# Moved fills, split waits, other banks and a changed order in a one-core transformer layer

## The chip, the core and the metric

One core of a Trainium2 chip runs one launch of a whole layer in f32. The metric is device time in microseconds (us). A core has TensorE (matmuls into eight banks of PSUM), VectorE, ScalarE and GpSimd (elementwise work), and SyncE (SP), which issues most transfers. Each works through its own queue in order and waits on semaphores.

## The reference, cut to what matters

1024 tokens of width 1024. After a layer norm, one projection feeds four token mixers A to D and four gates for each channel; each mixer's output is projected (`w_br_*`), weighted with its sigmoid gate, the four are added, and `w_out` follows. Then a layer norm (LN1), and a mixture of experts: each token takes 6 of 64 experts, and a shared expert runs for all.

```python
def hybrid_mixer(h, w_in, ...):
    proj = h @ w_in
    ...
    g = sigmoid(gate).reshape(bsz, seq, N_BRANCH, D_MODEL)
    merged = g[:,:,0]*(ya @ w_br_a) + g[:,:,1]*(yb @ w_br_b) + g[:,:,2]*(yc @ w_br_c) + g[:,:,3]*(yd @ w_br_d)
    return merged @ w_out

def forgetting_attention(q, k, v, f_logit):            # mixer D
    c = cumsum(log_sigmoid(f_logit))
    s = q @ k.T * HEAD_DIM ** -0.5 + c[query] - c[key]  # causal softmax, then @ v

def moe_ffn(h, ...):
    idx, w = route(xf, w_router, router_bias)           # top 4 of 8 groups, top 6 of 64
    routed = routed_experts(xf, idx, w, wg, wu, wd)     # silu(x @ wg) * (x @ wu) @ wd * w
    shared = (silu(xf @ sg) * (xf @ su)) @ sd
    return routed + shared
```

## The kernel before, in words

All order is written by hand: every engine has its own program, and semaphores tie them together. The stages are these.

**Projection in.** `norm_in_and_project` normalizes and turns the tokens, then projects. Six blocks of 256 columns are done with seven half-size products each instead of eight (`block_part(n, r)`, L767). These need sums of token halves, t1 to t4, which VectorE makes once (L663 to L668), and sums of weights, which GpSimd makes. The semaphore `tsum` counts the token sums.

**Mixers.** A, B, C and D run one after the other. Dense work lies between the small steps of each as a filler. In `mix_d` it is eleven gate units of seven products, each product four *parts* (`gate_part`, L1709): 308 parts in one list. `fill(8, "start")` does the first eight; then TensorE waits for mixer C's output to be read, for rows of ones, and for `drop_in`, the four small copies by SP that put the cumulated forget row into the keys. `score(u)` follows for 32 pairs of row tile and head, with `fill(4)` behind each score, 4 or 3 ahead of each `values`, and 2 within the turns that have two groups. What is left goes last, `fill(len(parts), "end")`. VectorE (`join`) and ScalarE (`copy`) read the products out of the banks, at points that the table `done` gives them from the same fills; GpSimd adds one of them (`crossed`) and makes the weight sums of the unit after next; SP stores the results in DRAM (`gates`, `spilled`) and loads the next weights.

**Merge.** A barrier of all engines. `merge` walks 64 gates in the order `order`: 60 come back from DRAM, four are projected here. SP first loads the four branch weights, a to d. Before the first branch product (L1957) TensorE projects two units and then waits for all four loads, `wbr` at 64.

**LN1, shared expert and routing.** Another barrier, then `norm_and_route`, for eight row tiles m. `mix(m, h)` (L2119) is `w_out`; its result stands in banks 0 and 1, and `mix(m, 0)` waits until VectorE has added tile m-1 into `base` (L2243). Then come the normalization, `turn`, `logits`, `count`, and the shared expert's `up`, `turn_hidden`, `down` (L2167, L2174, L2183), four or five tiles behind. On VectorE these have `hidden` (L2273) between up and turn_hidden, and `sum_base` (L2266) after down. At the stage's end the first experts' lists are made: TensorE `lists(b)` (L2598), VectorE `select` (L2923, what `lists` reads) and `index` (L2928 to L2945, which the gather on GpSimd reads). `turned_first` is the transpose (L2975) of the first gathered rows.

**Experts.** One `step(i, c)` for each expert, in four steps of their own, a loop of fifteen times four, and a tail. TensorE: `lists` of three experts on, `up` (L2982), `down` of the expert before (L2998), `turn_hidden` (L2990). VectorE: `take_rows`, `index`, `select`, `turned` (L2975), `hidden` (L2700), `result` (L2707), and in the first four steps one part each of `overflow_tables` (L2458 to L2477). SP loads an expert's three weights once `down` of four experts earlier has ended; experts 0 to 3 are loaded from `norm_and_route`, the fourth of them after its last `down`.

The order at the end of the routing stage is, on TensorE and on VectorE:

```python
lists(0); down(4); turn_hidden(5); up(6); lists(1); down(5); turn_hidden(6); up(7); lists(2); down(6); turn_hidden(7); down(7)
select(0); sum_base(3); index(0); select(1); hidden(5); sum_base(4); index(1); select(2); hidden(6); sum_base(5); index(2); select(3); hidden(7); sum_base(6); turned_first(); sum_base(7)
```

Of the kernel before, what the change touches and what calls it, by code (L numbers as in the profile page):

```python
# [26 lines left out]
ALU = mybir.AluOpType  # L27
# [3 lines left out]
P = 128  # L31
# [329 lines left out]
def norm_in_and_project(g):  # L361
# [74 lines left out]
    with nc.Block() as block:  # L436
# [181 lines left out]
        def _(dve):  # L618
# [42 lines left out]
            for c in range(2):  # L661
                dve.wait_ge(xT_read[c], KT)
            dve.tensor_tensor(t1, tok[0][1], tok[0][0], ALU.subtract).then_inc(tsum, 1)  # L663
            dve.tensor_tensor(t3, tok[1][1], tok[0][1], ALU.subtract).then_inc(tsum, 1)
            dve.wait_ge(tsum, 1)
            dve.tensor_tensor(t2, tok[1][1], t1, ALU.subtract).then_inc(tsum, 1)
            dve.wait_ge(tsum, 3)
            dve.tensor_tensor(t4, tok[1][0], t2, ALU.subtract).then_inc(tsum, 1)  # L668
            dve.wait_ge(lb1, 1)
            dve.reciprocal(oml[:], lb[:]).then_inc(lbd, 1)  # L670
# [45 lines left out]
        def _(pe):  # L716
# [30 lines left out]
            def block_part(n, r):  # L747
                (a11, a12), (a21, a22) = weights(n)
                s1, s2, s4 = sums(n)
                third = t3 if n < 4 else t3_late  # L750
                left, right, b, alone = ((a11, tok[0][0], 0, True), (a12, tok[1][0], 1, True), (s2, t2, 0, False),
                                         (s1, t1, 1, True), (a21, third, 0, False), (s4, tok[1][1], 1, False),
                                         (a22, t4, 0, False))[r]
                if r == 0:
                    loaded(pe, n)
                    pe.wait_ge(*((joined, 3 * n) if n else (g.proj_read, g.rows_unit - 1)))
                elif r == 1:
                    pe.wait_ge(*((copied, 4 * n) if n else (g.proj_read, g.rows_unit)))
                elif r % 2:
                    pe.wait_ge(joined, 3 * n + r // 2)  # L760
                else:
                    pe.wait_ge(copied, 4 * n + r // 2)
                if r == 2:
                    pe.wait_ge(wsum, 4 * n + 4)
                    pe.wait_ge(tsum, 4 if n < 4 else 5)
                for k in range(4):
                    mm = pe.matmul(block_bank(n, b), left[:, k, :], right[:, k, :], start=(alone and k == 0),  # L767
                                   stop=(k == 3), skip_group_check=True)
                mm.then_inc(prod, 1)
# [824 lines left out]
def mix_d(g):  # L1594
# [119 lines left out]
    def tensor(pe):  # L1714
# [5 lines left out]
            del parts[:count]  # L1720
            done[point] = 7 * GATES_D - (len(parts) + 3) // 4

        fill(8, "start")
        pe.wait_ge(g.c_yT_read, NT)
        pe.wait_ge(s["ones"], 2)
        pe.wait_ge(drop_in, 64)
# [177 lines left out]
def merge(g):  # L1904
# [8 lines left out]
    wbr, merged = g.region(WBR, 10, D), g.region(MERGED, KT, T)  # L1913
    sig = [g.region(WOUT + KT * D + HALF * i, HALF) for i in range(3)]
    tiles = [range(0, 4), range(4, 6), range(6, 8), range(8, 10)]
    s = {n: sem("m_" + n) for n in "wbr br sig prod sum".split()}
    gate_in = [sem(f"gate_in{i}") for i in range(3)]
    back = [0, 0, 0]
    wout_in = g.keep("wout_in")
# [7 lines left out]
    with nc.Block() as block:  # L1927
        @block.sync
        def _(sp):
            for a, w in zip(tiles, (g.ins["w_br_a"], g.ins["w_br_b"], g.ins["w_br_c"], g.ins["w_br_d"])):  # L1930
                sp.dma_start(wbr[:, a.start:a.stop, :], w[0].rearrange("(k p) n -> p k n", p=P)).then_inc(s["wbr"], 16)
            for p, v in enumerate(order):
                if p == 0:
                    sp.wait_ge(g.spilled, 16 * S)
# [9 lines left out]
        def _(pe):  # L1944
# [3 lines left out]
            for p, v in enumerate(order):  # L1948
                j, b, h = place(v)
                if v >= S and v not in ahead:  # L1950
                    project_unit(g, pe, unit[v], banks)
                if p == 0:
                    pe.wait_ge(s["wbr"], 64)
                if p >= 2:
                    pe.wait_ge(s["prod"], p - 1)
                for k in tiles[b]:
# [57 lines left out]
def norm_and_route(g, w):  # L2014
# [50 lines left out]
    g.exp_in = [g.keep(f"exp_in{i}") for i in range(4)]  # L2065
    flat2 = lambda a: bank[:, a:a + 2, :].rearrange("p b n -> p (b n)")
    up_bank = [5, 5, 5, 5, 1, 3, 1, 5]
    h_in = [sem(f"h_in{m}") for m in range(NT)]

    def sync(sp):  # L2070
# [40 lines left out]

    def tensor(pe, lists):
        def mix(m, h):
            if m:
                pe.wait_ge(s["sum"], m)
            for k in range(KT):
                if m == 0 and h == 0 and k == WOUT_K:
                    pe.wait_ge(s["wout"], 16 * (KT - WOUT_K))
                mm = pe.matmul(bank[:, h, :], merged[:, k, m * P:(m + 1) * P], wout[k][:, h * HALF:(h + 1) * HALF],  # L2119
                               start=(k == 0), stop=(k == KT - 1))  # L2120
            if h == 1:
                mm.then_inc(s["mix"], 1)
# [102 lines left out]
        lists(2)  # L2225
        down(6)
        turn_hidden(7)
        down(7)

    def vector(dve, select, index, turned_first):  # L2230
        step = [0]
# [7 lines left out]
        def norm(m):  # L2239
            z = base[:, m, :]  # L2240
            dve.wait_ge(s["mix"], m + 1)
            dve.wait_ge(h_in[m], 16)
            dve.scalar_tensor_tensor(out=z, in0=z, scalar=ALPHA, in1=flat2(0), op0=ALU.mult,  # L2243
                                     op1=ALU.add).then_inc(s["sum"], 1)
            dve.wait_ge(s["sum"], m + 1)
            for h in range(2):
# [108 lines left out]
        placed(7)  # L2355
        select(0)
        sum_base(3)
        index(0)
        select(1)
        hidden(5)  # L2360
        sum_base(4)
        index(1)
        select(2)
        hidden(6)
        sum_base(5)
        index(2)
        select(3)
        hidden(7)
        sum_base(6)
        turned_first()  # L2370
        sum_base(7)

    def scalar(act):
        def std(m):
# [124 lines left out]
def experts(g):  # L2499
# [61 lines left out]
    with nc.Block() as block:  # L2561
# [25 lines left out]
        def _(pe):  # L2587
# [35 lines left out]
            def step(i, c):  # L2623
                if has(i, c, 3):
                    lists(i, c + 3)
                up(i, c)
                if has(i, c, -1):
                    down(i, c - 1)
                turn_hidden(i, c)

            def ready():
# [28 lines left out]
        def _(dve):  # L2660
# [67 lines left out]
            def step(i, c):  # L2728
# [8 lines left out]
                hidden(i, c)  # L2737
                if has(i, c, -1):
                    result(i, c - 1)
                if isinstance(i, int) and i == 0:  # L2740
                    overflow_tables(g, dve, c, then, s["tabled"])

# [381 lines left out]
```

## Time and profile before

| what | us |
|---|---|
| timed runs, median of 3 (lowest to highest) | 2174.82 (2169.76 to 2176.11) |
| profiled execution, its own time | 2170.03 |
| its span in the trace | 2168.3 |
| TensorE busy | 2068.5 (95%) |
| VectorE busy | 1085.7 (50%) |
| GpSimd busy | 704.1 (32%) |
| ScalarE busy | 423.7 (20%) |

The stages as they lie in the span: the projection up to about 200 us, the mixers up to 973, the merge to 1143, LN1 and routing to 1374, experts to about 2118, then the last layer norm. A profile row gives an engine's busy time and, in brackets, the idle time before it and who ended that.
### The profile page before, as it was taken

Reading aid. Unit: us, or ns where it says so; the run is one execution under the profiler, and the core shown is the slowest. Engines: PE = TensorE matmul, PEld = TensorE weight load, DVE = VectorE, ACT = ScalarE, POOL = GpSimd, SP = SyncE. Lnnn points to the kernel's source line nnn. Section 1 sums busy time; section 2 is a strip of 40 time slices with the busy share of each in tenths; the row PEclk is TensorE's granted clock in tenths of the full one; section 3 lists DMA queues with packets and bytes.
Section 4 is the critical chain, followed back from the end, with each engine's and each line's share of the span. In section 5 each row is a group of like instructions: output and inputs, shape, how many; then the busy total and the mean of one; then the engine's idle time right before and its main releaser. Section 6 shows DMA issues by size and latency. Waiting matters only on the chain. (4 is left out here: it accounts for less than half of the span.)

```text
span 2168.3 us, 23007 instructions
## 1 busy us (share of the span) xinstructions
PE 2068.5 (95%) x7129; PEld 1091.5 (50%) x7130; DVE 1085.7 (50%) x2963; ACT 423.7 (20%) x909; POOL 704.1 (32%) x612
## 2 busy tenths in 40 slices
PE   7999999999999999999999999899999999999990
PEld 6445887574644555554444554344444444444440
DVE  6121444549451222212224756776666666666647
ACT  2111333334321111112221221011111111111112
POOL 1752002212032221203341001454455545555533
PEclk9999999999999999999999999999999999999995
DMA  5421000012112221216336004799999999999964
GB/s 142 117 88 39 20 21 20 20 45 73 45 49 78 68 78 44 73 54 232 102 98 213 30 39 164 263 342 344 351 351 358 361 359 357 348 358 350 348 196 156
DMA packets 129900, 368.23 MB, mean 170 GB/s; under 512 B 34332, under 2 KB 66192, under 8 KB 104352
## 3 DMA queue, kind: packets, MB, share of 16 engines
q1 hardware_dynamic: 104224, 312.64, 38.6%
q0 software_dynamic: 23520, 54.61, 10.5%
q8 instruction: 43, 0.70, 0.1%
q10 hardware_dynamic: 2080, 0.01, 0.1%
q14 instruction: 33, 0.27, 0.0%
HBM read 318.37 MB, written 68.16 MB: 178 GB/s over the span
## 5 line engine op out<-in xcount | busy, mean ns | idle before, releaser
L2982 PE MATMUL banks<-arena 128*128 128x512 f32 x1056 | 470.0, 598 | 3.0 <-DVE arena L2975 0.8
L2961 POOL DMA_INDIRECT arena<-h_rows,index x268 | 278.0, 1037 | 154.9 <-issue 75.7
L2982 PEld LDWEIGHTS banks<-arena 128*128 128x128 f32 x1056 | 195.7, 190 | 226.6 <-issue 225.4
L1709 PE MATMUL banks<-arena 128*128 128x512 f32 x616 | 281.4, 599 | 0.4 <-ACT arena L329 0.4
L2998 PE MATMUL banks<-arena 128*128 128x512 f32 x528 | 237.6, 592 | 1.3 <-ACT arena L2797 0.8
L285 PE MATMUL banks<-arena 128*128 128x512 f32 x480 | 220.2, 596 | 3.0 <-PEq L108 3.0
L2975 DVE STREAM_TRANSPOSE arena<-arena 128x1024 f32<-128x1024 f32 x66 | 133.9, 2028 | 131.0 <-PE banks L2982 131.0
L2969 POOL DMA_INDIRECT sums<-arena,row_to x66 | 107.1, 1622 | 271.1 <-DMA sums<-arena,row_to 251.5
L1709 PEld LDWEIGHTS banks<-arena 128*128 128x128 f32 x616 | 111.1, 191 | 117.3 <-issue 116.2
L2998 PEld LDWEIGHTS banks<-arena 128*128 128x128 f32 x528 | 100.2, 190 | 127.0 <-issue 125.3
L2945 DVE TENSOR_SCALAR index<-row 32x1 uint32<-32x1 f32 x1072 | 155.5, 145 | 17.1
L767 PE MATMUL banks<-arena 128*128 128x512 f32 x336 | 147.0, 599 | 2.2 <-DVE arena L682 2.2
L1957 PE MATMUL banks<-arena 128*128 128x512 f32 x320 | 138.4, 593 | 1.8 <-DMA arena<-in_w_br_d_dram 1.8
L291 PE MATMUL banks<-arena 128*128 128x256 f32 (+1 forms) x640 | 139.9, 360 | 0.0
L285 PEld LDWEIGHTS banks<-arena 128*128 128x128 f32 x480 | 86.7, 191 | 83.9 <-issue 82.7
L291 PEld LDWEIGHTS banks<-arena 128*128 128x128 f32 x640 | 108.6, 191 | 18.6 <-issue 1.3
L2119 PE MATMUL banks<-arena 128*128 128x512 f32 x256 | 112.9, 594 | 5.0 <-PEq L1927 3.0
L2792 ACT ACTIVATE arena<-banks 128x256 f32<-128x256 f32 x65 | 25.0, 384 | 433.2 <-PE banks L2982 433.2
L1986 DVE TENSOR_TENSOR arena<-arena,banks 128x512 f32<-128x512 f32 x64 | 44.0, 687 | 130.6 <-PE banks L1957 98.6
L767 PEld LDWEIGHTS banks<-arena 128*128 128x128 f32 x336 | 64.0, 192 | 83.7 <-issue 79.1
L1957 PEld LDWEIGHTS banks<-arena 128*128 128x128 f32 x320 | 60.4, 190 | 79.5 <-issue 69.1
L2707 DVE TENSOR_SCALAR arena<-banks,weight 128x512 f32<-128x512 f32 x64 | 48.0, 751 | 77.0 <-PE banks L2998 71.1
(392 smaller groups left out, 2383.3 us busy)
## 6 DMA issues: line engine op xcount, KB each, us to landing
arena<-in_w_exp_gate_dram SPq DMA_DIRECT2D x66, 1024.0 KB
arena<-in_w_exp_up_dram SPq DMA_DIRECT2D x66, 1024.0 KB
arena<-in_w_exp_down_dram SPq DMA_DIRECT2D x66, 1024.0 KB
arena<-in_w_in_dram SPq DMA_DIRECT2D x26, 1024.0 KB, 5.4
gates<-arena SPq DMA_DIRECT2D x60, 256.0 KB, 2.0
arena<-gates SPq DMA_DIRECT2D x60, 256.0 KB, 2.6
arena<-h_rows,index POOLq DMA_INDIRECT x268
arena<-in_x_dram SPq DMA_DIRECT2D x8, 512.0 KB, 5.7
```

Source lines behind the costliest of these rows:

```text
L285: mm = pe.matmul(bank[0:width], w[:, q, col:col + width], g.hT[:, q, at * HALF:(at + 1) * HALF], start=(q == 0), stop=(q == KT - 1))
L291: mm = pe.matmul(bank[:, m * width:(m + 1) * width], g.hT[:, k, (at + m) * P:(at + m + 1) * P], w[:, k, col:col + width], start=(k == 0), ...
L767: mm = pe.matmul(block_bank(n, b), left[:, k, :], right[:, k, :], start=(alone and k == 0), stop=(k == 3), skip_group_check=True)
L1709: mm = pe.matmul(gate_bank(n, b), left[:, k, :], right[:, k, :], start=(alone and k == 0), stop=(k == 3), skip_group_check=True)
L1957: mm = pe.matmul(bank[:, 4 + p % 2, :], wbr[:, k, j * P:(j + 1) * P], g.yT[:, k, h * HALF:(h + 1) * HALF], start=(k == tiles[b][0]), stop= ...
L2119: mm = pe.matmul(bank[:, h, :], merged[:, k, m * P:(m + 1) * P], wout[k][:, h * HALF:(h + 1) * HALF], start=(k == 0), stop=(k == KT - 1))
L2945: ins = dve.tensor_scalar(g.index[32 * b:32 * b + 32, k, q:q + 1], g.row[32 * q:32 * q + 32, k, :], 4.0, float(b), ALU.mult, ALU.add)
L2961: return pool.indirect_dma_start(w.x[k][:, 256 * q:256 * (q + 1)], None, rows, bass.IndirectOffsetOnAxis(ap=g.index[:, k, q:q + 1], axis=0 ...
L2969: return pool.indirect_dma_start(g.sums, bass.IndirectOffsetOnAxis(ap=g.row_to[:, b:b + 1], axis=0), w.y[k], None, bounds_check=last, oob_ ...
L2975: return dve.transpose(w.xT.rearrange("p k (q n) -> p q k n", q=4), w.x[k].rearrange("p (q n k) -> p q k n", q=4, k=KT))
L2982: mm = pe.matmul(g.bank[:, 2, :].rearrange("p (a f) -> p a f", a=2), xT[:, k, :], wgu[:, :, k, :], start=(k == 0), stop=(k == KT - 1))
L2998: mm = pe.matmul(g.bank[:, 4 + h, :], hidT[:, k, :], wdn[:, k, h * HALF:(h + 1) * HALF], start=(k == 0), stop=(k == 1))
```

## The change

1. First stage: VectorE makes t1, t2, t3, t4 instead of t1, t3, t2, t4, and t4 waits for two sums, not three. TensorE waits for t2 before product 2, for t3 before product 4, for t4 before product 6, instead of for all before product 2.
2. Mixer D: sixteen parts instead of eight ahead of the scores.
3. Merge: a semaphore for each branch's weights; each branch product waits for its own.
4. Mix of tile 1 goes to banks 6 and 7 and no longer waits for tile 0's sum.
5. Routing: on VectorE `hidden(5)`, `hidden(6)`, `hidden(7)` go ahead of the `index` and `select` that preceded them. `down(7)` goes into the first expert's step, behind `up`, and `sum_base(7)` there behind `hidden`.

```diff
@@ norm_in_and_project, vector
             dve.tensor_tensor(t1, tok[0][1], tok[0][0], ALU.subtract).then_inc(tsum, 1)
-            dve.tensor_tensor(t3, tok[1][1], tok[0][1], ALU.subtract).then_inc(tsum, 1)
             dve.wait_ge(tsum, 1)
             dve.tensor_tensor(t2, tok[1][1], t1, ALU.subtract).then_inc(tsum, 1)
-            dve.wait_ge(tsum, 3)
+            dve.tensor_tensor(t3, tok[1][1], tok[0][1], ALU.subtract).then_inc(tsum, 1)
+            dve.wait_ge(tsum, 2)
             dve.tensor_tensor(t4, tok[1][0], t2, ALU.subtract).then_inc(tsum, 1)
@@ block_part, tensor
                 if r == 2:
                     pe.wait_ge(wsum, 4 * n + 4)
-                    pe.wait_ge(tsum, 4 if n < 4 else 5)
+                if n == 0 and r in (2, 4, 6):
+                    pe.wait_ge(tsum, r // 2 + 1)
+                if n >= 4 and r == 4:
+                    pe.wait_ge(tsum, 5)
@@ mix_d, tensor
-        fill(8, "start")
+        fill(16, "start")
@@ merge
-    s = {n: sem("m_" + n) for n in "wbr br sig prod sum".split()}
+    s = {n: sem("m_" + n) for n in "br sig prod sum".split()}
+    wbr_in = [sem(f"wbr_in{b}") for b in range(4)]
@@ merge, sync
-            for a, w in zip(tiles, (g.ins["w_br_a"], g.ins["w_br_b"], g.ins["w_br_c"], g.ins["w_br_d"])):
-                sp.dma_start(wbr[:, a.start:a.stop, :], w[0].rearrange("(k p) n -> p k n", p=P)).then_inc(s["wbr"], 16)
+            for b, w in enumerate((g.ins["w_br_a"], g.ins["w_br_b"], g.ins["w_br_c"], g.ins["w_br_d"])):
+                a = tiles[b]
+                sp.dma_start(wbr[:, a.start:a.stop, :], w[0].rearrange("(k p) n -> p k n", p=P)).then_inc(wbr_in[b], 16)
@@ merge, tensor
-                if p == 0:
-                    pe.wait_ge(s["wbr"], 64)
+                pe.wait_ge(wbr_in[b], 16)
@@ norm_and_route
+    def mix_bank(m):
+        return 6 if m == 1 else 0
@@ mix(m, h), tensor
-            if m:
+            if m >= 2:
                 pe.wait_ge(s["sum"], m)
...
-                mm = pe.matmul(bank[:, h, :], merged[:, k, m * P:(m + 1) * P], wout[k][:, h * HALF:(h + 1) * HALF],
+                mm = pe.matmul(bank[:, mix_bank(m) + h, :], merged[:, k, m * P:(m + 1) * P], wout[k][:, h * HALF:(h + 1) * HALF],
@@ norm_and_route, tensor, its end
         turn_hidden(7)
-        down(7)
+        first.last_down = lambda: down(NT - 1)
@@ norm(m), vector
-            dve.scalar_tensor_tensor(out=z, in0=z, scalar=ALPHA, in1=flat2(0), op0=ALU.mult,
+            dve.scalar_tensor_tensor(out=z, in0=z, scalar=ALPHA, in1=flat2(mix_bank(m)), op0=ALU.mult,
@@ norm_and_route, vector, its end
         sum_base(3)
+        hidden(5)
         index(0)
         select(1)
-        hidden(5)
         sum_base(4)
+        hidden(6)
         index(1)
         select(2)
-        hidden(6)
         sum_base(5)
+        hidden(7)
         index(2)
         select(3)
-        hidden(7)
         sum_base(6)
         turned_first()
-        sum_base(7)
+        first.last_sum = lambda: sum_base(NT - 1)
@@ experts, tensor, step
                 if has(i, c, -1):
                     down(i, c - 1)
+                else:
+                    first.last_down()
                 turn_hidden(i, c)
@@ experts, vector, step
                 if has(i, c, -1):
                     result(i, c - 1)
+                else:
+                    first.last_sum()
```

## Rows read from the trace of the kernel before

**Rows 1.** The page, part 1: busy us (share of the span) and instructions.
```profile
PE 2068.5 (95%) x7129; PEld 1091.5 (50%) x7130; DVE 1085.7 (50%) x2963; ACT 423.7 (20%) x909; POOL 704.1 (32%) x612
```

**Rows 2.** TensorE's waits over the span: us in total, times, longest.
```profile
PE banks L1737 <- DMA arena<-arena: 4.2, 1, 4.2
PE banks L2174 <- DVE arena L2273: 3.9, 3, 1.3
...
PE banks L285 <- PEq L108: 3.0, 1, 3.0
...
PE banks L1957 <- DMA arena<-in_w_br_d_dram: 1.8, 1, 1.8
```

**Rows 3.** Timeline, VectorE in the first stage: start us, us, engine line op.
```profile
44.28 2.29 DVE L668 TENSOR_TENSOR arena<-arena 128x2048 f32<-128x2048 f32 x1
```

**Rows 4.** Timeline, TensorE around D's first score and the stage's end.
```profile
617.36 7.11 PE L1709 MATMUL banks<-arena 128*128 128x512 f32 x16 [0.43 <-ACT arena L329]
628.71 0.46 PE L1737 MATMUL banks<-arena 128*128 128x128 f32 x2 [4.25 <-DMA arena<-arena]
...
629.06 8.78 PE L1709 MATMUL banks<-arena 128*128 128x512 f32 x16
...
960.68 12.18 PE L1709 MATMUL banks<-arena 128*128 128x512 f32 x28
```

**Rows 5.** Three stretches: us, busy by engine, PEclk, DMA share, GB/s.
```profile
630.00:632.00 2.00, 2.00 (x4) 0.67 (x3) 0.00 (x0) 0.24 (x2) 1.95 (x2) 0.50 0.00 0
978.00:982.00 4.00, 4.00 (x11) 1.74 (x10) 0.00 (x0) 0.00 (x0) 0.00 (x0) 1.00 0.98 393
1384.00:1386.00 2.00, 1.75 (x12) 1.17 (x13) 1.90 (x5) 0.39 (x1) 1.00 (x1) 0.50 0.89 324
```

**Rows 6.** Timeline, ScalarE and VectorE ahead of D's first score.
```profile
622.24 0.60 ACT L1873 ACTIVATE arena<-banks 128x512 f32<-128x512 f32 x1 [2.32 <-DMA gates<-arena]
...
623.14 1.71 DVE L1798 TENSOR_SCALAR arena<-rows 8x1024 f32<-8x1024 f32 x1
624.78 0.66 DVE L1812 TENSOR_TENSOR arena<-arena,banks 128x512 f32<-128x512 f32 x1
```

**Rows 7.** DMA issues: KB each, median us to landing.
```profile
arena<-in_w_br_d_dram SPq DMA_DIRECT2D x1, 1024.0 KB, 13.3
```

**Rows 8.** Timeline, TensorE and VectorE at the first two tiles' mix.
```profile
1162.73 7.13 PE L2119 MATMUL banks<-arena 128*128 128x512 f32 x16 [1.37 <-DVE arena L2243]
...
1166.22 1.28 DVE L2260 SCALAR_TENSOR_TENSOR arena<-arena,rstd 128x1024 f32<-128x1024 f32 x1
```

**Rows 9.** Timeline, TensorE and VectorE from routing into the first experts.
```profile
1370.95 3.67 PE L2183 MATMUL banks<-arena 128*128 128x512 f32 x8 [0.78 <-DVE arena L2266]
...
1384.25 0.70 PE L2990 MATMUL banks<-ident,arena 128*128 128x128 f32 x2 [2.47 <-DVE arena L2700]
...
1385.00 8.31 PE L2982 MATMUL banks<-arena 128*128 128x512 f32 x16
...
1396.58 0.39 PE L2990 MATMUL banks<-ident,arena 128*128 128x128 f32 x2
...
1340.90 2.52 DVE L2945 TENSOR_SCALAR index<-row 32x1 uint32<-32x1 f32 x16
1343.46 1.22 DVE L2923 TENSOR_TENSOR arena<-iota,arena 128x1024 bf16<-128x1024 f32 x1
...
1370.72 2.03 DVE L2975 STREAM_TRANSPOSE arena<-arena 128x1024 f32<-128x1024 f32 x1
...
1384.11 0.28 DVE L2458 TENSOR_TENSOR_SCAN arena<-arena 128x64 f32<-128x64 f32 x1
...
1393.42 2.03 DVE L2975 STREAM_TRANSPOSE arena<-arena 128x1024 f32<-128x1024 f32 x1 [0.47 <-PE banks L2982]
1395.38 0.38 DVE L2700 TENSOR_TENSOR arena<-arena,banks 128x256 f32<-128x256 f32 x1
```

**Rows 10.** The expert loop's stretch, columns as in rows 5.
```profile
1450.00:2025.00 575.00, 572.96 (x1767) 271.44 (x1766) 378.93 (x1300) 70.02 (x156) 293.71 (x259) 1.00 1.01 353
```

## The prediction, made before the change was run

> **What bounds the kernel.** The page comes first: TensorE is busy 2068.5 us of 2168.3, the other engines half of it or less [rows 1]. So a change pays only where TensorE waits, or where its clock is low. The list of TensorE's waits comes next [rows 2]; I set each edit beside the wait it could touch. Then the timelines around these waits and the granted clock after them [rows 3 to 9]. In the expert loop, 575 us of it, TensorE is busy 572.96 us, while the 16 DMA engines are occupied throughout [rows 10]. That last row is the one to worry about, and has a rival of its own.
>
> The profiled execution took 2170.03 us (span 2168.3 and 1.7 around it). The three timed runs have a median of 2174.82, 4.8 us more. I work out a difference against the profile and take it off the median. 0.3%, about what a measurement of this kernel can tell from no change, is 6.5 us.
>
> **Token sums, first stage.** The order of two subtractions of equal size is swapped, and TensorE waits for t2, t3 and t4 separately. The fourth ends at 46.6 us [rows 3], while TensorE is in the projections before the block products for 8 us more; no wait on them is in the list. That work is their cover. Cost and gain 0. If that cover were gone, waiting separately would give at most two subtractions.
>
> **Sixteen parts ahead of D's scores.** Eight parts (16 records, since an f32 part shows as two) take 7.11 us and end at 624.47. Then TensorE is idle 4.25 us for the four copies of the drop row into the keys, and the score starts at 628.71 [rows 4]. The granted clock is 0.50 afterwards (1.2 GHz) [rows 5], and the next sixteen records take 8.78 us instead of 7.11, so 1.67 more are lost [rows 4].
> The change puts eight more parts before the score: products 2 and 3 of the first gate unit. At 0.43 us a record (the fourteen parts at the stage's end: 28 records in 12.18 [rows 4]) they take 6.9 us and end at 631.4. The score's condition holds since 628.7, so the wait is gone and no new one is there. Can they start? Product 2 needs the copy of product 0, which ends at 622.84; product 3 needs the join of product 1, which ends at 625.44, 2.5 us before its turn; the last token sum ends where the drop begins, at 623.14 [rows 6]. What is late next: VectorE joins product 3 (0.66 us) before the first maximum, and ScalarE copies product 2 (0.60) before the first exponential. TensorE has four parts (3.43 us) to do meanwhile, as it has now. GpSimd and the stores on SP's queue keep their order. The work is the same and the fill at the end of the stage falls from fourteen parts to six; the loop's fills stay full. What waited behind the last fill, the cross sum and stores of the last unit, has its inputs earlier. The barrier's 3.0 us stay. Term: -4.25 - 1.67 = -5.9. Bounds: -4.25 if something else lowers the clock there; 0 if the wait returns in the first score steps.
>
> **Branch weights one by one.** TensorE waits 1.8 us for branch D's weights [rows 2]. The first product of the merge is a unit not stored in DRAM, which sorts first, and its branch is D, whose transfer is issued last and lands 13.3 us after issue [rows 7]. So the first product waits for the same transfer: 0. The added waits, some sixty, are already met and stand ahead of the wait on the previous product, where the queue stands anyway: 0, and at most 0.1 us for the first two, which have none.
>
> **Mix of tile 1 in banks 6 and 7.** TensorE waits 1.37 us for VectorE to read tile 0's sum out of the banks [rows 8]. With other banks it goes on. The next thing, turning tile 0, needs VectorE's result, which stands 6.1 us after the wait's start (1167.5 against 1161.4); the half mix in front takes 6.9, so 0.8 us remain. From tile 2 on the wait was hidden by logits and stays. Term: -1.4; bounds 0 and -1.4.
>
> **Routing stage.** Three waits, 3.9 us together, are for `hidden` [rows 2], which VectorE does after `index` (16 spreads, 2.52 us) and `select` (1.22) though its input is ready before them [rows 9]. In the new order it comes first, so I lay the steps out anew, on the old time axis. lists(0) at 1339.88, down(4) 1340.1 to 1343.5, no wait, up(6) to 1350.6, down(5) 1350.8 to 1354.3, no wait, up(7) to 1361.4, down(6) to 1365.0, turn_hidden(7) to 1365.3. VectorE: hidden(7) 1362.4, index(2) to 1365.6 (3.2 with its three small steps), select(3) to 1366.8, sum_base(6) to 1367.9, the first transpose (2.03) to 1369.95. Before, down(7) (3.43 of its 3.67) covered exactly this chain. It is now moved behind up(0,0), so a new wait appears: 1.5 us before lists(3), then 2.9 before up(0,0).
> up(0,0) 1370.0 to 1376.9, down(7) to 1380.35. VectorE needs 2.03 + 0.4 after up(0,0) for the second transpose and hidden(0,0): 1379.3, under the cover of down(7). So the old wait of 2.47 and the slow up(0,1) behind it (8.31 for 7.11, clock 0.50) [rows 5, 9] go.
> Now VectorE sets the pace. sum_base(7) (1.2) stands behind hidden(0,0) and ends at 1381.7; the overflow tables start there, against 1384.11. In the old trace hidden(0,1) ended 11.65 us after that start, 0.47 of it idle [rows 9], so it ends at 1392.9 and TensorE waits 1.6 us for it. The old step turned hidden at 1396.58: -3.8. The idle microsecond VectorE then had goes too and the following steps, VectorE-bound, keep -4.1.
> Against it stands the clock. The new 4.4 us of waiting are about as long as the 4.25 that halved it. 2.47 halved it as well, while the 3.0 us of a barrier left it at 1.00 [rows 2, 5]. Too mixed for a rule, so I go by the nearest row, 4.25, and by what the halved stretches cost, 1.20 and 1.67: c = 1.4, passed on since both chains hang on up(0,0). Term: -4.1 + 1.4 = -2.7. Bounds: -4.1 (full clock) and -0.8 (two halved stretches of 1.67, the second after the wait of 1.6).
> SP's queue: expert 3's three loads now leave at 1381, 6 us later; needed at about 1406. At the loop's 353 GB/s [rows 10] its 3.1 MB need 9 us: 15 to spare. The store of sum 7 follows; the first scatter waits for it until about 1393 and is ready at 1396. Behind that scatter on GpSimd stands only the gather for expert 5, needed at 1424. Cost 0.
>
> **Sum.** -5.9 - 1.4 - 2.7 = -10.0: the profiled execution would be 2160.0, the median 2164.8.
>
> **Rivals.**
> *Transfers pace the experts.* What is gained before the loop comes back as waits in it. For it: the DMA share of 1.01 over 575 us at 353 GB/s [rows 10]. Against it: TensorE idles 2.04 us there (575 - 572.96), the list of waits has no transfer of expert weights, and elsewhere transfers ran faster than that [rows 5]. If all is given back, 2174.8. The Trainium skill's Perfetto Trace Analysis, sections Engine Utilization and What "DMA-bound" means, would call the loop memory-bound: 353 is 99% of the 358 GB/s it gives a core. By that rule the time is 2174.8, not 2164.8. The same page adds that a lone core can draw more than this share, and that the busy share of matmuls flatters TensorE.
> *The loop turns slower (other side).* The same engines, another phase: expert 3's weights come 6 us later and expert 4's 5 earlier, and gathers and scatters meet the loads differently. If a transpose then waits for its gather in each of 60 steps by 0.17 us, the 10 us are gone; from 0.28 us a step (10 + 6.5, over 60) the kernel is slower by over 0.3%: 2181.4. Against it: the loop's waits name no gather today, and its four buffers absorb a shift of one load.
> *D's wait moves.* The parts in front delay the first scores and TensorE waits in the first steps instead. -1.4 - 2.7: 2170.7. Against it: every input above is 1.3 us or more ahead.
> *down(7) in its new place gains nothing.* A longer wait than 4.4 and a second halved clock: -7.3, 2167.5; still faster.
>
> **Chances.** Forecast 0.62, range of its own 2159 to 2168. Transfers give back all or most 0.10; loop slower 0.05; D's wait moves 0.10; down(7) gains nothing 0.13. Faster by over 0.3% means below 2168.3: forecast 0.59 of its 0.62, 0.11 of the down(7) case, 0.03 of D's: 0.73. Slower 0.05, within 0.22. The range leaves out the slower case and most of the given-back one, and reaches below to a full clock in routing and a median as near the fastest run as the profiled one: 2158 to 2173.
>
> **What would show it.** D: score(0) at about 631.4 without a wait, no 0.50 around 630 to 633, stage end 5.9 us earlier. Merge: a wait of 1.8 us for branch D, as before. Mix: no wait of 1.37. Routing: no waits at the three turn_hidden, a new one of 1.5 and 2.9 around lists(3), one of about 1.6 at the second expert's turn_hidden, 0.50 in up(0,0). The forecast is wrong if the loop's stretch grows over 575 us, or if a wait for a transfer appears at the experts' up-products.

## The result and the profile after

The changed kernel takes 2160.67 us (median of 5 runs, 2158.75 to 2163.20), the kernel before beside it 2173.92 (5 runs, 2169.76 to 2176.11). The ratio is 0.9944, with a 95% interval of 0.9930 to 0.9958: 12.2 us less (9.1 to 15.2). The forecast, 10.0 less, lies in the interval. The profiled execution took 2160.67 us, with a span of 2158.9: 9.4 less than the 2168.3 of before.

The page: TensorE's busy time is 0.7 us more than before [rows 1], so what this pair of profiles gains is idle time that went.

```profile
PE 2069.2 (96%) x7129; PEld 1093.2 (51%) x7130; DVE 1086.9 (50%) x2963; ACT 423.6 (20%) x909; POOL 703.4 (33%) x612
```

The list of TensorE's waits, as [rows 2]:

```profile
PE banks L2993 <- DVE arena L2986: 3.5, 2, 2.7
...
PE banks L285 <- PEq L108: 3.0, 1, 3.0
PE banks L3001 <- DVE arena L2709: 2.2, 3, 1.5
...
PE banks L2605 <- DVE arena L2934: 1.3, 1, 1.3
...
PE banks L1961 <- DMA arena<-in_w_br_d_dram: 1.0, 1, 1.0
```

The 4.2 for the drop row, the three turn_hidden waits of 3.9 together and the 1.4 for tile 0's sum have gone; 2.7 and 1.3 are new. Line numbers after the change are 3 to 11 higher: L1712 is the gate part, L2993 `up`, L3001 the turn of the experts' hidden, L2986 the transpose.

Timeline, TensorE at mixer D's start and at the merge's start, as [rows 4]:

```profile
615.06 13.97 PE L1712 MATMUL banks<-arena 128*128 128x512 f32 x32 [0.43 <-ACT arena L329]
628.87 0.38 PE L1740 MATMUL banks<-arena 128*128 128x128 f32 x2
...
629.14 7.09 PE L1712 MATMUL banks<-arena 128*128 128x512 f32 x16
...
967.39 15.67 PE L285 MATMUL banks<-arena 128*128 128x512 f32 x32 [3.01 <-PEq L108]
984.04 1.12 PE L1961 MATMUL banks<-arena 128*128 128x512 f32 x2 [0.98 <-DMA arena<-in_w_br_d_dram]
```

The score starts with no idle time before it, and the parts behind it take 7.09 us, not 8.78. From the first part to the first product behind the barrier it is 967.39 - 615.06 = 352.33 us; before it was 975.88 - 617.36 = 358.52. So the stage is 6.2 shorter. But the 32 records behind the barrier take 15.67 us; those of before took 13.97, after a wait of the same 3.0.

Timeline, TensorE at the first two tiles' mix, as [rows 8]:

```profile
1138.59 22.54 PE L2126 MATMUL banks<-arena 128*128 128x512 f32 x48 [3.21 <-PEq L1931]
1160.97 1.04 PE L2136 MATMUL banks<-ident,arena 128*128 128x128 f32 x8
```

Three half mixes run as one row, with no wait of 1.37 in it.

Timeline, TensorE from routing into the experts, as [rows 9], then VectorE in the same stretch:

```profile
1358.19 0.38 PE L2181 MATMUL banks<-ident,arena 128*128 128x128 f32 x2
1359.89 0.35 PE L2605 MATMUL banks<-arena 128*128 128x6 bf16 x8 [1.31 <-DVE arena L2934]
1362.94 9.54 PE L2993 MATMUL banks<-arena 128*128 128x512 f32 x16 [2.69 <-DVE arena L2986]
...
1375.74 0.39 PE L3001 MATMUL banks<-ident,arena 128*128 128x128 f32 x2
...
1376.17 7.11 PE L2993 MATMUL banks<-arena 128*128 128x512 f32 x16
...
1388.19 0.51 PE L3001 MATMUL banks<-ident,arena 128*128 128x128 f32 x2 [1.47 <-DVE arena L2709]
```

```profile
1359.75 1.22 DVE L2273 SCALAR_TENSOR_TENSOR arena<-arena,banks 128x1024 f32<-128x1024 f32 x1
1360.88 2.00 DVE L2986 STREAM_TRANSPOSE arena<-arena 128x1024 f32<-128x1024 f32 x1
```

turn_hidden(7) (1358.19) has no wait. Then TensorE waits 1.31 us for `select`, and 2.69 more while VectorE does sum_base(6) and the first transpose. `up`, 7.11 us elsewhere, takes 9.54. down(7) behind it covers the second transpose, and the first turn of an expert's hidden (1375.74) no longer waits.

Stretches with the clock, columns as in [rows 5, 10]:

```profile
48.00:50.00 2.00, 2.00 (x11) 2.00 (x10) 1.07 (x4) 0.78 (x2) 1.85 (x2) 0.50 0.95 393
...
630.00:632.00 2.00, 2.00 (x6) 0.95 (x5) 0.14 (x1) 0.46 (x2) 1.50 (x2) 1.00 0.00 0
...
970.00:972.00 2.00, 2.00 (x4) 0.90 (x3) 0.00 (x0) 0.00 (x0) 0.00 (x0) 0.53 0.98 389
...
1140.00:1142.00 2.00, 2.00 (x4) 0.93 (x3) 1.34 (x2) 0.00 (x0) 1.94 (x8) 0.50 0.85 340
...
1314.00:1316.00 2.00, 2.00 (x4) 0.86 (x3) 1.76 (x16) 0.90 (x1) 0.00 (x0) 0.50 0.96 297
...
1362.00:1364.00 2.00, 1.06 (x2) 0.55 (x3) 1.86 (x8) 0.00 (x0) 1.39 (x3) 0.50 1.10 303
...
1425.00:2000.00 575.00, 572.85 (x1762) 270.77 (x1761) 377.79 (x1296) 68.90 (x154) 292.60 (x258) 1.00 1.01 354
```

The first of these stretches in the kernel before:

```profile
48.00:50.00 2.00, 2.00 (x20) 2.00 (x19) 0.42 (x2) 1.49 (x2) 1.24 (x1) 1.00 0.63 264
```

At 630 the clock is full now. It is half in five other places. Two of them, at 48 and at 970, have the same work and no longer idle time ahead of them than before, when the clock was full there. The stretch at 48 came instead of one: before, the first stage had its half clock at 92, behind a wait of 2.2 us that is 1.1 here. The last row is the experts' loop: 572.85 us busy of 575, as before.

### The profile page after: what moved, and what is told of

It is laid out like the page before. It is cut to its first block and busy times, and to the rows that moved or that the text cites. A ratio compares the mean times of both kernels' runs of the same rounds, so it can differ in the third digit from the quotient of the medians.

```text
span 2158.9 us, 23073 instructions
## 1 busy us (share of the span) xinstructions
PE 2069.2 (96%) x7129; PEld 1093.2 (51%) x7130; DVE 1086.9 (50%) x2963; ACT 423.6 (20%) x909; POOL 703.4 (33%) x612
## 5 line engine op out<-in xcount | busy, mean ns | idle before, releaser
L2993 PE MATMUL banks<-arena 128*128 128x512 f32 x1056 | 471.2, 599 | 5.8 <-DVE arena L2986 3.5
L2993 PEld LDWEIGHTS banks<-arena 128*128 128x128 f32 x1056 | 196.2, 191 | 230.2 <-issue 226.2
L1712 PE MATMUL banks<-arena 128*128 128x512 f32 x616 | 279.7, 596 | 0.4 <-ACT arena L329 0.4
L2986 DVE STREAM_TRANSPOSE arena<-arena 128x1024 f32<-128x1024 f32 x66 | 133.9, 2028 | 135.2 <-PE banks L2993 135.2
L1712 PEld LDWEIGHTS banks<-arena 128*128 128x128 f32 x616 | 110.5, 190 | 116.1 <-issue 115.1
L2956 DVE TENSOR_SCALAR index<-row 32x1 uint32<-32x1 f32 x1072 | 155.4, 145 | 17.1
```

The costliest lines, as they stand in the source:

```text
L1712: mm = pe.matmul(gate_bank(n, b), left[:, k, :], right[:, k, :], start=(alone and k == 0), stop=(k == 3), skip_group_check=True)
L2956: ins = dve.tensor_scalar(g.index[32 * b:32 * b + 32, k, q:q + 1], g.row[32 * q:32 * q + 32, k, :], 4.0, float(b), ALU.mult, ALU.add)
L2986: return dve.transpose(w.xT.rearrange("p k (q n) -> p q k n", q=4), w.x[k].rearrange("p (q n k) -> p q k n", q=4, k=KT))
L2993: mm = pe.matmul(g.bank[:, 2, :].rearrange("p (a f) -> p a f", a=2), xT[:, k, :], wgu[:, :, k, :], start=(k == 0), stop=(k == KT - 1))
```

## The experiments

The parts were put into the kernel before one by one (the two edits of waits together). Then came five variants, and two kernels were run again. All ratios are to the kernel before on the same chip; us are the ratio less 1, times the median of before.

| kernel | ratio (95%) | us against before | span |
|---|---|---|---|
| changed | 0.9944 (0.9930 to 0.9958) | -12.2 | 2158.9 |
| changed, run again | 0.9950 (0.9937 to 0.9964) | -10.9 | 2160.3 |
| fill 16 alone | 0.9976 (0.9967 to 0.9986) | -5.2 | 2163.1 |
| mix banks alone | 0.9997 (0.9988 to 1.0007) | -0.7 | 2168.8 |
| routing alone | 0.9987 (0.9978 to 0.9996) | -2.8 | 2165.7 |
| only `hidden` earlier | 0.9982 (0.9972 to 0.9992) | -3.9 | 2166.8 |
| split waits alone | 1.0003 (0.9991 to 1.0015) | +0.7 | 2169.6 |
| fill 24 alone | 0.9962 (0.9948 to 0.9975) | -8.3 | 2166.0 |
| changed, idle time filled | 0.9943 (0.9931 to 0.9956) | -12.4 | 2157.7 |
| changed, first turn earlier | 0.9929 (0.9917 to 0.9941) | -15.4 | 2156.6 |
| the same, branch D's weights first | 0.9927 (0.9914 to 0.9940) | -15.9 | 2155.5 |
| that one again | 0.9928 (0.9914 to 0.9941) | -15.7 | 2151.7 |

**Sixteen parts alone.**

```diff
-        fill(8, "start")
+        fill(16, "start")
```

> The kernel before with the second part of the change alone: sixteen parts ahead of D's scores. Theory: the 4.25 us of waiting and the 1.67 us of half clock behind it go, so about 6 us less, ratio 0.9972; the stretch from the first part to the second score is 14.3 us for twenty-four parts and one score. Rival (D's wait moves): a wait of some us appears within the first scores and the time is within 1 us of before. Second rival: the waits themselves go, but half-clock stretches of 1.7 us fall elsewhere, so the difference is 6 plus or minus 1.7 or 3.4.

Measured 5.2 us less (3.0 to 7.2). Timeline, TensorE:

```profile
615.81 13.97 PE L1709 MATMUL banks<-arena 128*128 128x512 f32 x32 [0.44 <-ACT arena L329]
629.62 0.38 PE L1737 MATMUL banks<-arena 128*128 128x128 f32 x2
...
629.90 7.08 PE L1709 MATMUL banks<-arena 128*128 128x512 f32 x16
```

The wait and the slow records behind it are gone here too, and nothing else of the change is in this kernel. This part carries about half of the gain. From the first part to the second score it is 21.0 us: the 14.3 that was expected is about what sixteen parts and a score take, not twenty-four.

**Mix banks alone.**

```diff
-            if m:
+            if m >= 2:
                 pe.wait_ge(s["sum"], m)
...
-                mm = pe.matmul(bank[:, h, :], ...)
+                mm = pe.matmul(bank[:, mix_bank(m) + h, :], ...)
```

> The kernel before with tile 1's mix in banks 6 and 7 alone. Theory: 1.4 us less, ratio 0.9994, which the measurement cannot tell from 1; in the trace no wait of 1.37 us before the second mix, and the turn of tile 0 follows its half mix without a wait. Rival: the turn of tile 0 waits for VectorE instead and nothing is gained.

Measured 0.7 less, from 2.6 less to 1.5 more: the ratio can't tell 1.4 from nothing. Timeline, TensorE:

```profile
1150.18 15.72 PE L2122 MATMUL banks<-arena 128*128 128x512 f32 x36 [0.68 <-DMA arena<-in_w_out_dram]
1165.73 1.04 PE L2132 MATMUL banks<-ident,arena 128*128 128x128 f32 x8
```

The wait of 1.37 is gone, so the edit does what it says. From the first mix to the first turn of a tile (L2132) it is 21.62 us, against 23.29 before. But the stretch from there to lists(0) is 3.4 us longer (173.55 against 170.18), with two half-clock stretches behind the last tile's logits.

**Routing alone.** Edit 5 of the change: `hidden` earlier, down(7) and sum_base(7) moved into the first step.

> The kernel before with the routing part alone (hidden ahead of index and select, and down(7) and sum_base(7) moved into the first expert's step). Theory: as the trace of the changed kernel shows, 4.1 us less minus what the longer half clock after the new 4.0 us of waiting costs (2.4): 1.7 less, ratio 0.9992. Rival (full clock there): 4.1 less, 0.9981. The wait before lists(3) is 1.3 and the one before up(0,0) 2.7 in either.

Measured 2.8 less (0.9 to 4.8). Timeline, TensorE:

```profile
1366.44 0.35 PE L2598 MATMUL banks<-arena 128*128 128x6 bf16 x8 [1.32 <-DVE arena L2927]
1369.49 8.83 PE L2986 MATMUL banks<-arena 128*128 128x512 f32 x16 [2.69 <-DVE arena L2979]
...
1394.03 0.51 PE L2994 MATMUL banks<-ident,arena 128*128 128x128 f32 x2 [1.47 <-DVE arena L2702]
```

The three new waits are those of the changed kernel within 0.01 us. The slow `up` took 8.83 us here and 9.54 there. The waits repeat, the granted clock behind them does not.

**Only `hidden` earlier,** down(7) and sum_base(7) left in their old places:

```diff
+        hidden(5)
         index(0)
         select(1)
-        hidden(5)
```

and the same for hidden(6) and hidden(7).

> The kernel before with only the new order of hidden on VectorE; down(7) and sum_base(7) stay where they were. Worked out by the same steps: the three waits of 1.3 go, down(7) then waits 2.6 us for sum_base(6), up(0,0) starts 3.1 us earlier, the wait of about 2.5 before the first expert's turn_hidden and its half clock stay. Theory: 3.1 us less, ratio 0.9986, so more than e3 by 1.4 if moving down(7) costs a longer half clock, less than e3 by 1.0 if it doesn't.

Measured 3.9 less (1.7 to 6.1). Timeline, TensorE:

```profile
1369.45 5.14 PE L2183 MATMUL banks<-arena 128*128 128x512 f32 x8 [2.54 <-DVE arena L2266]
...
1384.23 0.51 PE L2990 MATMUL banks<-ident,arena 128*128 128x128 f32 x2 [2.48 <-DVE arena L2700]
```

down(7) now waits 2.54 us for sum_base(6), where it waited 0.78 before, and takes 5.14 us for 3.67, at a half clock. The 2.48 ahead of the experts' first turn stay. From the start of lists(0) to the sixth turn of an expert's hidden it is 101.01 us; with down(7) moved as well, 101.20; before, 103.63. So in these two traces the order of `hidden` gives what the routing edit gives, and moving down(7) adds nothing. The two ratios can't tell them apart either.

**Split waits alone** (token sums, branch weights).

> The kernel before with the token sums' order and waits and the branch weights' four semaphores alone. Theory: nothing, ratio 1.0000 within the measurement; TensorE still waits 1 to 2 us for branch D's weights, the last issued and the first needed. Rival: the three other parts alone gave 5.2, 0.7 and 2.8 us in ratios, 8.7 together against 12.2 for the whole change, so 3 us could sit here; then some wait of the first stage or of the merge is shorter by that.

Measured 0.7 more, from 2.0 less to 3.3 more: no difference. From the first branch product to the first mix, where the sixty added waits stand, it is 154.55 us, against 154.79 before.

**The idle time filled.** In the changed kernel TensorE does one unread f32 product into bank 4 after turn_hidden(7) and three after lists(3), ahead of up(0,0). They are added work, read by nobody.

```diff
+        def idle_products(count):
+            for _ in range(count):
+                pe.matmul(bank[:, 4, :], wgu[:, 0, 0:P], wgu[:, 0, :], start=True, stop=True)
```

> The changed kernel with four products that nobody reads in the new wait of the routing stage: one behind turn_hidden(7), three between lists(3) and up(0,0), 3.4 us of the 4.0 that TensorE is idle there. They add work but delay nothing by more than 0.1 us. Theory (the idle time is what lowers the clock): the up-product of the first expert takes 7.1 us instead of 9.5, and everything behind it comes 2.4 us earlier. Rival (the half clock falls there for another reason): it stays at 8.8 to 9.5.

Measured 12.4 less than before (9.6 to 15.0). Timeline, TensorE:

```profile
1361.11 0.35 PE L2612 MATMUL banks<-arena 128*128 128x6 bf16 x8 [0.46 <-DVE arena L2943]
1361.32 2.82 PE L2238 MATMUL banks<-arena 128*128 128x512 f32 x6
1364.18 7.13 PE L3002 MATMUL banks<-arena 128*128 128x512 f32 x16
```

With the same VectorE chain and the idle time taken up, `up` takes 7.13 us, where the three executions with the idle time had 9.54, 9.69 and 8.83. So the idle time ahead of it is what lowered the clock, as far as one execution can tell. From lists(0) to the sixth turn it is 99.46 us, against 101.81. The ratio doesn't resolve these 2.4 us.

**The first turn earlier.** On VectorE the transpose of the first expert's rows goes ahead of hidden(7).

```diff
         sum_base(5)
+        turned_first()
         hidden(7)
         index(2)
         select(3)
         sum_base(6)
-        turned_first()
```

> The changed kernel with the first gathered rows' transpose ahead of hidden(7) on VectorE, which is idle there for 4.9 us, instead of behind sum_base(6). Theory: lists(3) still waits 1.3 us for select(3), but the wait of 2.7 before up(0,0) goes, down(7) now covers the second transpose only in part (a wait of 0 to 0.2), and with no half clock the first expert's turn_hidden comes 5.3 us earlier than in the changed kernel; the overflow steps keep that lead. Ratio to before 0.992. Rival: VectorE waits for the gather of expert 0, hidden(7) comes late, and nothing is gained.

Measured 15.4 less than before (12.8 to 18.0). Timeline, TensorE:

```profile
1361.17 0.35 PE L2605 MATMUL banks<-arena 128*128 128x6 bf16 x8 [1.32 <-DVE arena L2934]
1361.38 7.11 PE L2993 MATMUL banks<-arena 128*128 128x512 f32 x16
...
1384.22 0.51 PE L3001 MATMUL banks<-ident,arena 128*128 128x128 f32 x2 [1.47 <-DVE arena L2709]
```

VectorE in the same kernel:

```profile
1351.35 2.02 DVE L2986 STREAM_TRANSPOSE arena<-arena 128x1024 f32<-128x1024 f32 x1
1356.36 0.42 DVE L2280 TENSOR_TENSOR arena<-arena,banks 128x256 f32<-128x256 f32 x1 [2.99 <-ACT arena L2404]
```

The transpose went into time in which VectorE was idle (4.93 us ahead of its L2280 in the changed kernel, 2.99 here). The 2.69 are gone, and 1.32 alone was not followed by a half clock, here or in the two executions of the next kernel. lists(0) to the sixth turn is 96.59 us, 5.2 less than in the changed kernel, and these are the 2.69 and the 2.43 that the slow `up` cost. The 1.47 at the second turn stay: there VectorE is the slower one.

**The same with branch D's weights issued first.**

```diff
-            for b, w in enumerate((g.ins["w_br_a"], g.ins["w_br_b"], g.ins["w_br_c"], g.ins["w_br_d"])):
-                a = tiles[b]
+            for b in (3, 0, 1, 2):
+                a, w = tiles[b], g.ins[f"w_br_{'abcd'[b]}"]
```

> The same with branch D's weights issued ahead of the other three in the merge. Theory: they land some 5 us after issue and the wait of 1 to 2 us at the first branch product goes; branch A's, now second, lands before the second product. 1.5 us less than the run before, ratio 0.9913. Rival: the wait moves to the second product, for branch A's 2 MB.

Measured 15.9 less than before (13.0 to 18.7). DMA issue of branch D's weights (KB, us to landing), then the timeline of TensorE:

```profile
arena<-in_w_br_d_dram SPq DMA_DIRECT2D x1, 1024.0 KB, 6.3
```

```profile
969.46 15.67 PE L285 MATMUL banks<-arena 128*128 128x512 f32 x32 [3.02 <-PEq L108]
984.97 10.46 PE L1961 MATMUL banks<-arena 128*128 128x512 f32 x24
```

They land 6.3 us after issue, not 13.3 [rows 7], and the first branch product waits for nothing. It starts 15.5 us after the first product behind the barrier in both executions of this kernel, where sixteen parts with the old order of issue had 16.0 to 17.1. The ratio shows 0.5 us less than the run before, where 1.5 was expected, and the intervals overlap. From lists(0) to the sixth turn it is 97.90 us here and 97.96 in the second execution. That is 1.3 more than the run before, with a half-clock stretch at 1406 and 1404. So the first product waited for its own branch's transfer alone. The split of the semaphore bought nothing by itself; it lets the order of issue take the wait away.

**The changed kernel once more.**

> The changed kernel itself, once more. If the sum of the single parts (5.2 + 0.7 + 2.8 - 0.7 = 8.0 us less) and the difference of the two profiled spans (9.4) are nearer the truth than the first ratio (12.2), this run gives about 9 us less, ratio 0.9957; if the first ratio is right, 0.9944 again, and then the parts together are worth more than alone. Waits in the trace as in the first profile: 1.3, 2.7 and 1.5 us.

0.9950, 10.9 less: between the two, and it tells nothing apart. Timeline, TensorE:

```profile
968.15 13.97 PE L285 MATMUL banks<-arena 128*128 128x512 f32 x32 [3.02 <-PEq L108]
985.23 15.29 PE L1961 MATMUL banks<-arena 128*128 128x512 f32 x35 [3.11 <-DMA arena<-in_w_br_d_dram]
```

What it does show is that the same instructions after the same 3.0 us ran at full clock this time (13.97, not 15.67), and the wait for branch D was 3.11, not 0.98. The weights set that start, so in this kernel a half clock ahead of them costs nothing.

**Twenty-four parts alone.** `fill(24, "start")` in the kernel before.

> The kernel before with 24 instead of 8 dense parts ahead of mixer D's scores and nothing else. The scores' wait was already gone with 16 parts, so if it was the wait that the parts paid for, eight more buy nothing: ratio as with 16 (0.9976, 5 us less), the score products without a wait, but the end of the stage 8 parts shorter, where a wait may open for up to 8 x 0.44 = 3.5 us (then 2 us less). If instead more products without a break hold the clock in the rest of the stage, it is 7 us less or better.

Measured 8.3 less (5.4 to 11.3), where sixteen parts gave 5.2 (3.0 to 7.2). The expectation has one sum wrong: eight parts are sixteen records and take 6.9 us, not 3.5. Timeline, TensorE:

```profile
637.09 0.38 PE L1737 MATMUL banks<-arena 128*128 128x128 f32 x2
...
968.04 16.40 PE L285 MATMUL banks<-arena 128*128 128x512 f32 x32 [2.32 <-PEq L108]
```

From the first part to the first product behind the barrier it is 351.63 us against 352.33, and these 0.7 lie in the barrier's idle time (2.32 against 3.01). The forecast wait at the stage's end didn't come, nor did a clock that holds: it was half behind the barrier, as with sixteen. So the trace bears out 0.7 us of the 3.1; whether the rest is real stays open, since the intervals overlap.

**The best version once more.**

> The changed kernel with branch A's turn moved ahead of hidden(7) on VectorE and branch D's weights issued first, beside the changed kernel on the same chip. By the wait of 2.7 us and the half-clock stretch of 2.4 us behind it that the early turn takes away, and 1.0 us at branch D, up to 6 us less than the changed kernel; by the first two ratios (0.9944 and 0.9927) 3.7 us less.

What moved ahead of hidden(7) is the transpose of the first expert's rows, as in the two kernels above; "branch A's turn" is a slip. Measured 2157.29 us (5 runs, 2153.49 to 2159.49), beside 2162.12 for the changed kernel on the same chip: 4.8 less, between the 3.7 and the 6 expected. Both pairs of ratios point the same way, though the intervals of the ratios still overlap (0.9941 and 0.9937).

## Why the prediction was right

The profiled executions, taken together, give each step a size of its own. The table cuts them at points of the same work (differences of start times in TensorE's timeline) and takes the mean over the executions that have the step's old form and over those with its new one.

| piece | old form, mean (lowest to highest; executions) | new form | difference | forecast |
|---|---|---|---|---|
| start to mixer D's first part | 616.3 (615.0 to 617.4; 6) | 616.0 (614.9 to 617.1; 7) | -0.3 | 0 |
| to the first product of the merge | 358.9 (358.5 to 359.7; 5) | 352.3 (all; 7) | -6.5 | -5.9 |
| to the first branch product | 15.9 (15.7 to 16.0; 5) | 16.7 (16.0 to 17.1; 5) | +0.8 | 0 |
| to the first mix | 154.5 (154.1 to 154.8; 6) | 154.5 (154.1 to 154.7; 7) | 0.0 | 0 |
| to the first turn of a tile | 23.2 (22.3 to 24.0; 6) | 21.8 (20.7 to 22.4; 7) | -1.4 | -1.4 |
| to lists(0) | 170.8 (170.2 to 171.9; 6) | 172.1 (171.9 to 173.6; 7) | +1.4 | 0 |
| to the experts' sixth turn | 105.0 (103.6 to 106.9; 5) | 101.7 (101.2 to 102.0; 3) | -3.3 | -2.7 |
| to the end | 725.1 (724.3 to 725.6; 5) | 724.6 (724.2 to 725.1; 3) | -0.5 | 0 |

The differences add up to -9.8. Form here is the start fill for the second and third piece, the split waits for the first and fourth, the mix banks for the fifth and sixth, the routing edit for the last two. The executions with 24 parts, with D's weights first, with only `hidden` earlier, with the earlier turn or with the filled idle time are left out where they would mix. That the sum lies so near the forecast of -10.0 is in part luck: two pieces that were put at nothing cost 0.8 and 1.4, and the other pieces gave about as much more than forecast.

- **Token sums: 0, right.** Together with the branch weights' waits they made no difference, and the first piece spreads by 2.4 us in either form.
- **D's fill: -5.9, right, with its mechanism.** Score(0) came 14 us after the first part, without a wait; the idle time and the slow records are gone. The rival that the wait moves is out: the pieces are 352.33 us in all seven executions.
- **Branch weights: 0, right for the edit, wrong for the piece.** Sixty waits cost nothing, and D's transfer still ended the wait. But with sixteen parts ahead the weights land later: 15.3 us after issue in the changed kernel and 15.5 with the fill alone, against 13.3 [rows 7]. That gives back 0.8 us. One execution with sixteen parts (the earlier turn) had 13.2 again, so it isn't fixed, and what delays the transfer is open.
- **Mix: -1.4, right where the edit stands, and lost again behind it.** From the first mix to the first turn the new form takes 1.4 less. From there to lists(0) it takes 1.4 more. The step that failed is the one that ended the account at tile 2 ("the wait was hidden by logits and stays") and put the clock behind that at nothing. The last tile's logits wait 1.8 us for VectorE in all thirteen executions, and a half clock can follow. Timeline, TensorE, first mix, first turn and last logits with the `up` behind them, the kernel before and then the changed one:

```profile
1146.41 5.39 PE L2119 MATMUL banks<-arena 128*128 128x512 f32 x12 [2.96 <-PEq L1927]
...
1169.70 1.04 PE L2129 MATMUL banks<-ident,arena 128*128 128x128 f32 x8
...
1320.08 1.97 PE L2143 MATMUL banks<-arena 128*128 128x64 f32 x16 [1.75 <-DVE arena L2329]
1321.89 7.08 PE L2167 MATMUL banks<-arena 128*128 128x512 f32 x16
```

```profile
1311.36 1.98 PE L2150 MATMUL banks<-arena 128*128 128x64 f32 x16 [1.76 <-DVE arena L2336]
1313.17 8.78 PE L2174 MATMUL banks<-arena 128*128 128x512 f32 x16
```

The slow `up` costs 1.7 us. It stands there in all seven executions with the new banks, and in two of six without (only `hidden` earlier, fill 24 alone). So the pieces from the first turn to lists(0) are 170.2 us without it, 171.9 with it, and 173.6 in mix banks alone, which had two such stretches. Why it falls there more often behind the edit stays open: no run changes that wait, and two executions had it without the edit. The ratio can't tell whether the whole is worth 1.4 or nothing; its interval alone is -2.6 to +1.5.
- **Routing: -2.7, right; the clock term was mis-sized.** The waits were 1.31, 2.69 and 1.47 us, where 1.5, 2.9 and 1.6 had been worked out. The start of up(0,0) came 4.7 us earlier against lists(0) than in the profile of before, as laid out. Then c, the cost of the half clock, was 2.43 instead of 1.4 (2.58 in the second profile, 1.72 with routing alone), and -4.1 + 2.4 = -1.7 against the profile of before, whose piece was 103.63 (measured: 101.81, so -1.8). That profile was a lucky one: four others with the old order had 103.9 to 106.9, and in three of them (fill 16, split waits and fill 24 alone) down(7) itself took 5.37 us for 3.67, behind its wait of 0.78 [rows 9]. Against their mean the edit gives 3.3. The Trainium skill's TensorE: Matmul & The Clock Gate, section "Part 1: The HAM clock gate", says that the number of slow matmuls at a kernel's start varies between runs of the same kernel. Here it varies in the midst of one: the changed kernel's two traces have 13.97 and 15.67 us for the same records behind the same 3.0 us.
- **The rivals.** Transfers that pace the experts would have shown as a loop that gives the lead back. The loop is busy 572.85 of 575 us, the stretch behind the sixth turn did not grow, and all of the gain is still there at the end: out, and so is the slower loop. The Trainium skill's Perfetto Trace Analysis, section Engine Utilization, gives a core 358 GB/s of memory bandwidth as its 100%, and adds that a core can pull more where only one is active. The traces bear out the second: a stretch at 970 moved 389 GB/s, and the loop at 354 cost nothing of the lead. "down(7) gains nothing" is true in part: moving it bought nothing over the earlier `hidden` (101.20 against 101.01 us), because the wait that it covered came back ahead of up(0,0). The second half clock of that rival, behind the wait of 1.47, didn't come.
- **9.4 or 12.2.** The first ratio is 2.8 us better than the profiles' difference. The profile of before holds three half-clock stretches ahead of 2100 us, that of the changed kernel five. Cut by pieces over all executions the change is worth 9.8, the second ratio says 10.9, and the four single parts 8.0 (-5.2 - 0.7 - 2.8 + 0.7). The four half intervals, squared and added, make 4.4 around the 8.0, so it reaches into both ratios' intervals, and 9.8 lies in both. No gain from the parts' being together is shown, and none is ruled out.

## What to carry to other kernels

Take a wait away where the waiting engine is also slowed behind it, and count both: here 4.25 us of idle time cost 5.9. Before a covering piece of work is moved, look what its old place covered: the earlier `hidden` alone gave as much as with down(7) moved as well, and the step that paid was to put the chain's last link (the first transpose, 2.0 us) into VectorE's idle time. When the terms are 1 to 3 us in 2170, cut several executions at points of the same work and compare the pieces; one pair of profiles can be off by more than a term. Cut them right behind the edit too: the mix banks gave their 1.4 us there, and a piece that ended at lists(0) showed nothing.

## What the runs showed of the hardware

- The granted clock fell to 0.50 (1.2 GHz) at 46 to 52 us in the changed kernel, in projections that had no idle time ahead of them; the engine had just done sixteen records on 32 rows, as before. In the kernel before the same place ran at 1.00. Each of the thirteen executions had a half clock in one of two places of the first stage: at 46 to 54 us in four (changed, mix banks, split waits, best version again), at 92 to 98 in nine. There it stood right behind a wait of 2.2 us, which was 0.2 to 1.1 where the half clock had come early.
- Behind the idle time of the barrier ahead of the merge it fell in none of the five executions with eight parts, in six of the seven with sixteen, and in the one with 24. The idle time was 3.0 us, and 2.3 with 24. Why the parts matter there is not shown.
- One such stretch costs 1.7 us (15.67 against 13.97). After 1.31 and 2.69 us of idle time with little between them the cost was 1.7, 2.4 and 2.6 in three executions.
- A wait of 0.8 us behind three of 1.3 was followed by a slow down(7) in three of five executions (5.37 us for 3.67). 1.32 us of idle time alone, in the three executions with the earlier turn, was followed by an `up` of 7.11 us at full clock.
